# The lead-in of two expert layers: norm by halves, modulation shared with ScalarE, the second head's queries and choice moved forward, tile 1's norm later

## The reference

```python
x = layer_norm(alpha * x + gate1 * mixer(x * (1 + scale1) + shift1))
x = layer_norm(alpha * x + gate2 * peer_ffn(x * (1 + scale2) + shift2))
```

```python
s1, s2 = scores of the two query halves against 128 keys each
v1, i1 = top_k(s1, 16); v2, i2 = top_k(s2, 16)
top_s, pos = top_k(all 256 sums v1 + v2, 16)     # 16 of 16384 experts
gate = softmax(top_s)
act = gelu(dot(t, u_tab[idx]))
out += sum over the 16 of gate * act * v_tab[idx]
```

## Time and profile before

| | |
|---|---|
| runs, median (lowest to highest) | 1878.3 us (1877.2 to 1880.09), 3 runs |
| profiled execution, its own time | 1873.58 us |
| its span, first to last instruction | 1871.8 us |
| mean granted clock of TensorE | 0.980 |
| busy: PE, DVE, ACT, POOL | 1659.1, 1467.1, 601.9, 484.1 us |
| first gather, last gather, layer 0 | 379.56, 1025.13 us |
| first gather, last gather, layer 1 | 1212.25, 1844.74 us |

### The profile page before, as it was taken

How to read it: one execution, slowest core, us unless ns; L and a number is a source line. 1 busy time by engine, 2 the same in 40 slices (tenths; PEclk the granted TensorE clock), 3 DMA queues, 4 the chain that set the end, 5 groups by cost and what they waited for, 6 DMA issues and landing times.

```text
span 1871.8 us, 18240 instructions
## 1 busy us (share of the span) xinstructions
PE 1659.1 (89%) x5432; PEld 907.8 (48%) x5432; DVE 1467.1 (78%) x3511; ACT 601.9 (32%) x1495; POOL 484.1 (26%) x517
## 2 busy tenths in 40 slices
PE   8999999989999987889899998979999878787786
PEld 3787588445544433334343776545454423232332
DVE  6888996787677778898887799787787788777755
ACT  4565854123222223333322111032222323222221
POOL 0000000033333333343343000033333333333341
PEclk9999999999999999999999999989999999999999
DMA  8331239889999999999999685599999999999996
GB/s 356 138 128 59 113 138 370 347 307 420 427 419 427 427 425 417 389 425 427 424 416 428 268 310 225 198 417 422 428 426 426 427 426 419 420 420 426 418 421 273
DMA packets 95846, 664.33 MB, mean 355 GB/s; under 512 B 11357, under 2 KB 13374, under 8 KB 16388
## 3 DMA queue, kind: packets, MB, share of 16 engines
q0 software_dynamic: 73728, 536.90, 68.8%
q1 hardware_dynamic: 22020, 126.27, 17.4%
HBM read 662.02 MB, written 1.11 MB: 354 GB/s over the span
## 4 chain that ended last, share of the span: by engine, by line
PE 34%; DMA 25%; DVE 21%; issue 4%; ACT 2%; PEld 1%; DVEq 0%; POOL 0%; PEldq 0%; POOLq 0%; ACTq 0%
DMA expert_rows<-in_p_uv,chosen_experts 24%; PE bank L1181 19%; DVE dot_products L2497 7%; PE bank L966 3%; PE bank L1139 3%; PE bank L1041 2%; DVE silu_c_row_and_products L1885 1%; PE bank L1392 1%; ACT weight_diagonal L1721 1%; PE bank L981 1%; PEld bank L1181 1%; PE bank L1080 1%; PE bank L1295 1%; PE bank L1211 1%; PE bank L1218 1%
## 5 line engine op out<-in xcount | busy, mean ns | idle before, releaser
L1181 PE MATMUL bank<-expert_rows,weight_diagonal 128*128 128x512 f32 x2048 | 958.1, 612 | 165.3 <-ACT weight_diagonal L1721 163.5
L1432 POOL DMA_INDIRECT expert_rows<-in_p_uv,chosen_experts x512 | 483.7, 945 | 1361.0 <-PE bank L1181 775.8
L2497 DVE SCALAR_TENSOR_TENSOR dot_products<-expert_rows,bank 128x1024 f32<-128x1024 f32 x512 | 625.0, 1221 | 236.0 <-DMA expert_rows<-in_p_uv,chosen_experts 220.9
L1181 PEld LDWEIGHTS bank<-expert_rows,weight_diagonal 128*128 128x128 f32 x2048 | 379.9, 193 | 674.3 <-issue 390.8
L1721 ACT ACTIVATE weight_diagonal<-constants,expert_weights 128x128 f32<-128x128 f32 x512 | 177.8, 394 | 246.0 <-DVE expert_weights L2429 236.8
L1713 ACT ACTIVATE expert_gelu<-expert_dots 128x2 f32<-128x2 f32 x258 | 52.3, 203 | 613.2 <-DVE dot_products L2497 609.6
L926 PE MATMUL bank<-mixer_input_T_hi,weights_hi 128*128 128x512 f32 (+1 forms) x192 | 74.9, 390 | 7.9 <-DVE weights_lo L630 4.7
L2070 DVE SCALAR_TENSOR_TENSOR conv_work_or_state<-conv_work_or_state,channel_vectors 128x252 f32<-128x252 f32 (+2 forms) x192 | 71.9, 429 | 4.0 <-ACT conv_work_or_state L1541 3.9
L926 PE MATMUL bank<-mixer_input_T_hi,weights_lo 128*128 128x512 f32 (+1 forms) x192 | 72.8, 379 | 0.0
L926 PE MATMUL bank<-mixer_input_T_lo,weights_hi 128*128 128x512 f32 (+1 forms) x192 | 72.6, 378 | 0.0
L1311 PE MATMUL bank<-hyena_input_T,hyena_weight_block 128*128 128x256 f32 x320 | 70.5, 379 | 0.0
(11 more groups left out here) (330 smaller groups left out, 1906.3 us busy)
## 6 DMA issues: line engine op xcount, KB each, us to landing
weight_block<-in_ada_rows SPq DMA_DIRECT2D x22, 1024.0 KB, 6.4
weight_block<-in_m_in_blocks SPq DMA_DIRECT2D x20, 1024.0 KB, 6.0
hyena_weight_block<-in_ada_rows SPq DMA_DIRECT2D x15, 1024.0 KB, 7.1
hyena_weight_block<-in_h_in_blocks SPq DMA_DIRECT2D x12, 1024.0 KB, 6.8
weight_block<-in_wq_blocks SPq DMA_DIRECT2D x11, 1024.0 KB, 7.9
expert_rows<-in_p_uv,chosen_experts POOLq DMA_INDIRECT x512
out_weights<-in_m_out_blocks SPq DMA_DIRECT2D x6, 1024.0 KB, 8.1
weight_block<-in_ada_shift SPq DMA_DIRECT2D x4, 1024.0 KB, 11.3
```

The source lines that it names most:

```text
L1181: last = mm(ps[b][:, :], dg[n % DIAG][:, :], uv[slot][:, D + h * 512:D + (h + 1) * 512], start=(r == 0 and k == 0), stop=end)
L1432: pool.indirect_dma_start(uv[slot][:, :], None, A[f"p_uv{l}"], bass.IndirectOffsetOnAxis(ap=chosen[:, s_, k:k + 1], axis=0)).then_inc(uv_l ...
L2497: stt(prod[:, :], uv[slot][:, 0:D], 1.0, rows_t, ALU.mult, ALU.mult, accum_out=dots[:, s_, k + j:k + j + 1]).then_inc(sem("dots_done"), 1)
```

## The change

It has five parts, in both layers unless said.

1. **Halves in the first norm.** The last three row blocks of tile 0's output product are taken half by half, so that bank 0 ends two products ahead of bank 1. VectorE's gate, sum and statistics of half 0 stand ahead of those of half 1. The normalization and the transposes go by halves, with a semaphore for each half. In layer 0 two of the eight modulation dot products move behind the modulation of tile 0 (`LATE_DOTS`), and with them SP's later loads.
2. **ScalarE's share.** ScalarE modulates the second half of tile 0 and both halves of tile 1 (`modulate_half`); VectorE keeps the first half of tile 0. VectorE reads the first head's scores directly from the bank, so ScalarE's two copies go.
3. **The second head's queries at once.** A common `first_head` puts token rows and the second head's queries and scores ahead of most of tile 1's products. In layer 1 the gate rows move behind them all.
4. **The second head's choice** comes ahead of the first unit (pieces 0 to 3), behind the first dot product (4 and 5), and behind the first pair (6 and 7; in layer 1 behind tile 1's norm).
5. **Tile 1's norm later.** In layer 1 it moves behind the second pair of units, as in layer 0; its transposes stand ahead of the combine of unit 4 in both layers (before: of unit 2 in layer 0, of unit 0 in layer 1). In layer 1 the slots of the row buffers are turned by six, so that the first two gathers use buffers that don't wait for the products.

The core of the diff:

```diff
-        mixer_out(0, 0, 6)
+        out_steps = [(k, h) for k in range(INNER // P) for h in range(2)]
+        out_steps_first = out_steps[:-6] + [(k, h) for h in range(2) for k in range(INNER // P - 3, INNER // P)]
...
         def tile_transposes(l, t):
-            pe.wait_ge(sem("layer_norms_done"), TT * 2 * l + t + 1)
             for j in range(2):
+                pe.wait_ge(sem("norm_halves"), 2 * (TT * l + t) + j + 1)
...
+        def first_head(l, out_, steps):
+            out_(1, steps[0:4])
+            tile_transposes(l, 0)
+            out_(1, steps[4:5])
+            first_queries(l, 0, 0, 0, KD)
+            first_queries(l, 0, 1, 0, 4)
+            first_half_scores(l, 0)
+            first_queries(l, 0, 1, 4, KD)
+            token_rows(l, 0, (0,))
+            first_half_scores(l, 1)
+            token_rows(l, 0, (1,))
+            for c in range(2):
+                second_queries(l, 0, c, 0, KD)
+            out_(1, steps[5:7])
+            second_scores(l, 0)
+            out_(1, steps[7:])
...
+        first_head(1, hyena_out, hyena_steps)
         gate_rows(1, 1)
...
-                    if l == 0 and s_ == 0 and k == 2:
-                        tile_transposes(0, 1)
+                    if s_ == 0 and k == 4:
+                        tile_transposes(l, 1)
...
     # GpSimd
                     if n >= UVR:
                         pool.wait_ge(sem("combined"), n - UVR + 1)
+                        if n == UNITS + UVR - FIRST_SLOT[1]:
+                            wait_full(pool, ("hout", 3))
...
-        wait_full(pool, ("hout", 3))
         peer(1)
...
     # ScalarE
+            def modulate_half(t, j):
+                b = wait_full(act, ("tT", l, t, j))
+                for c in range(4):
+                    k = 4 * j + c
+                    last = f(tT[:, k, t * P:(t + 1) * P], ps[b][:, c * P:(c + 1) * P], ACT.Identity, scale=ada[l][:, 4, k:k + 1], bias=ada[l][:, 3, k:k + 1])
+                last.then_inc(read[b], 1)
...
+                    if s_ == 0 and k == (4, 2)[l]:
+                        for j in range(2):
+                            modulate_half(1, j)
...
     # VectorE: ln_stats
+            gated(0)
+            if t == 0:
+                added(0)
+            gated(1)
+            if t:
+                added(0)
+            after(added(1))
...
     # VectorE: choose_first
+                for a in range(2):
+                    b = wait_full(dve, ("sc0", l, 0, a))
+                    scored = ps[b][:, a * P:(a + 1) * P]
+                    after(step(V.max(topv[:, a, 0:8], scored)))
+                    step(V.max_index(topi[:, a, 0:8], topv[:, a, 0:8], scored))
+                    V.match_replace(left[:, a, :], topv[:, a, 0:8], scored, LOWEST).then_inc(read[b], 1)
+                    wait_read(dve, ("sc0", l, 0, a))
+                    after(best(topv[:, a, :], topi[:, a, :], None, left[:, a, :], True))
...
     # VectorE: the units
                 if s_ == 0:
+                    for piece in range(4):
+                        choose(1, piece)
                     gates_of(0)
...
+                        if s_ + k + j == 0:
+                            for piece in (4, 5):
+                                choose(1, piece)
...
-                    if l == 0 and s_ == 0 and k == 2:
+                    if s_ == 0 and k == 2:
                         second_tile()
+                        if l:
+                            for piece in (6, 7):
+                                choose(1, piece)
...
     # SP
-        weights(at("ada1_rows", 6), at(("wq", 0), 3) + 1)
-        ln_rows(0, 0)
+        weights(at("ada1_rows", 6), at(("wq", 0), 2) + 1)
         for h in range(2):
             wait_full(sp, ("gate", 0, 1, h))
         weights(0, 1, query_rings[0])
+        wait_full(sp, ("mout", 1))
+        sp.dma_start(fc[:, 0:FC_COLS], A["filter_constants"]).then_inc(sem("filter_in"), 16)
+        weights(at(("wq", 0), 3), at(("wq", 0), 3) + 1)
+        ln_rows(0, 0)
         wait_read(sp, ("mout", 0))
```

More of the change, by code:

```diff
@@ L88 @@
 UVR = 8
+FIRST_SLOT = (0, UVR - 2)
+LATE_DOTS = 2
 DIAG = 8
@@ L381, in plan_peer @@
         work_, sums = (2, 0) if l else (0, 2)
-        for t in range(TT):
+        for t in range(TT - l):
             for j in range(2):
@@ L391, in plan_peer @@
             plan.use(("sc1", l, 0) if r == 1 else ("sc", l, r, *tiled), 6 + r % 2)
+            if l and r == 1:
+                for h in range(2):
+                    plan.use(("gate", 1, 1, h), 2 + h)
+                for j in range(2):
+                    plan.use(("tT", l, 1, j), 6 + j)
             if l == 0 and r == 3:
@@ L491, in build_in @@
     plan_inv(1, 1)
-    for h in range(2):
-        plan.use(("gate", 1, 1, h), 2 + h)
     for j in range(4):
@@ L1117, in second_scores, with token_rows @@
             last.then_inc(full[b], 1)
-        def token_rows(l, t):
-            for h in range(2):
+        def token_rows(l, t, halves_=(0, 1)):
+            for h in halves_:
                 b = begin(("tn", l, t, h))
@@ L1237, in peer @@
                         filter_products((s_ - PH) // 2, s_ % 2, k)
-                    chunks = ((4, 6, 8, 10), (2, 5, 8, 11))[l] if s_ == 0 else (0, 1, 2, 3)
+                    chunks = (4, 6, 8, 10) if s_ == 0 else (0, 1, 2, 3)
                     if l == 0 and r in BY_TILE:
@@ L1772, in peer @@
                         copy_second_scores(1)
-                    if l == 0 and s_ == 0 and k == 2:
-                        ln_root(0, 0, 1)
-                    if s_ + 2 < PH and k == (10 + 2 * l if s_ == 0 else 4):
+                    if s_ == 0 and k == 2:
+                        ln_root(l, 0, 1)
+                    if s_ == 0 and k == (4, 2)[l]:
+                        for j in range(2):
+                            modulate_half(1, j)
+                    if s_ + 2 < PH and k == (10 if s_ == 0 else 4):
                         copy_queries(s_ + 2)
-                    if s_ + 2 < PH and k == (12 + 2 * l if s_ == 0 else 6):
+                    if s_ + 2 < PH and k == (12 if s_ == 0 else 6):
                         copy_scores(s_ + 2)
@@ L1910, in gate_diagonal, with modulate_tile @@
                ada[l][:, GATES[j], :].unsqueeze(2).to_broadcast([P, KD, P]), ALU.mult).then_inc(sem("gate_diagonals"), 1)
-        def modulate_tile(key, dsts, l, pair, t):
-            for j in range(2):
+        def modulate_tile(key, dsts, l, pair, t, banks_=(0, 1)):
+            for j in banks_:
                 b = wait_full(dve, key + (t, j))
@@ L2301, in ln_norm @@
             after(m)
-            ts(xres[:, t, :], xres[:, t, :], small[:, t, 12:13], small[:, t, 16:17], ALU.subtract, ALU.mult).then_inc(sem("layer_norms_done"), 1)
+            if j:
+                ts(xres[:, t, :], xres[:, t, :], small[:, t, 12:13], small[:, t, 16:17], ALU.subtract, ALU.mult).then_inc(sem("layer_norms_done"), 1)
+            else:
+                for h in range(2):
+                    x = xres[:, t, h * 512:(h + 1) * 512]
+                    ts(x, x, small[:, t, 12:13], small[:, t, 16:17], ALU.subtract, ALU.mult).then_inc(sem("norm_halves"), 1)
         def ln_apply(l, j, t):
@@ L2326, in _ @@
         gate_diagonal(0, 1)
-        for m in range(KD, 2 * KD):
+        for m in range(KD, 2 * KD - LATE_DOTS):
             modulation_dot(1, m)
@@ L2332, in peer @@
         def peer(l, keys):
-            modulate_tile(("tT", l), tT, l, 1, 0)
+            modulate_tile(("tT", l), tT, l, 1, 0, (0,))
+            if l == 0:
+                for m in range(2 * KD - LATE_DOTS, 2 * KD):
+                    modulation_dot(1, m)
             def best(val, idx, src, rest, second):
```

126 lines of the change are left out of this document (39 added, 87 removed).

## The result

The changed kernel takes 1884.6 us (median; 1882.4 to 1885.4), the kernel before, timed with it, 1878.5. The ratio is 1.0037, with an interval of 1.0028 to 1.0046: 0.37% slower, 12 us over the forecast and outside its range. The profiled execution took 1883.73 us (span 1881.9, before 1871.8). The traced execution of the kernel before lies 4.9 us under the median given here, the new one 0.9 under its own, so the two traces lie some 4 us further apart than the medians do.

What follows compares the result with a forecast made beforehand. Fixed-byte DMA plateaus of expert-row gathers bound the kernel, so an earlier stream start moves their end. Gains of 3.7 us in layer 0 and 2.4 in layer 1, together 6.1, take the median from 1878.3 to 1872.2 us; range 1867 to 1877.

Steps and rivals of the forecast that it cites:

- The 2.23 us ahead of the transposes: Layer 0, TensorE: norm by halves removes this idle time, so transposes can start at 360.7.
- the queries wait: Layer 0, TensorE: first queries wait 0.2 us for tile 0's modulated first half, 362.9 against TensorE free at 362.8.
- the second head's 0.77: Layer 0, TensorE: second head's queries wait 0.9 us (0 to 2) for the bank of scores VectorE reads itself.
- combine 4 starts: Layer 0, TensorE: starts at 405.3 instead of 410.39, so the thirteenth gather is issued at 407.2 instead of 412.65.
- The price that the Trainium skill gives for reading a bank: VectorE's direct score reads: skill implies 0.4 us more per layer, time 0.8 later; prediction took at most 0.04 each as nothing.
- the 2.4 us set against them: Layer 1's start: gain by 1260, taken between 3.2 us and 1.9 us with half a gather of unexplained shortfall.
- its rival: Only the start moves: layer 1's two gathers ahead (5.0) less the third's delay gives 1.8 us; chance 0.20.
- its second term: Layer 1's gain of 2.4 us, from two gathers near 1207 and the third issued at 1215.4.
- The step that failed: Layer 1: tile 1's norm delays combines of units 4 on, but not past the stream's need; buffers last until 1237.
- the prediction's signs of being wrong: TensorE's combines waiting for diagonals at 410, idle above 3 us before second queries, or a lower-rate plateau.
- Only the start moves: Rival: something else keeps buffers late behind the products; gain 0.9 plus 1.8, together 2.7 us, 1875.6; chance 0.20.
- The bank that VectorE must empty: Rival: TensorE waits before second queries in each layer; gain 6.1 - 2d, gone at d = 3.1; chance 0.08.

Runs made afterwards that it cites:

- kernel 4: Changed kernel with layer 1's orders, banks, copies and first buffer as before, so mainly layer 0's lead-in changed; 0.9982 of the kernel before.
- kernel 10: Changed kernel with only ScalarE's modulation of tile 1 in layer 1 moved behind the diagonals of units 4 and 5; 1.0010 of the kernel before.
- Kernel 12: Changed kernel with layer 1's norm a pair sooner, third head's copies later, last two choice pieces behind units 2 and 3; 0.9968 of the kernel before, median 1869.8 us.
- kernel 5: Changed kernel with, in layer 1, tile 1's norm a pair sooner and the third head's copies later, banks shared; 0.9963 of the kernel before.
- kernel 6: Changed kernel with, in layer 1, tile 1's norm a pair sooner, the third head's copies later and separate accumulator banks; 0.9970 of the kernel before.
- kernel 8: Changed kernel with layer 1's late norm kept, separate banks, third head's copies later, last two choice pieces and modulation behind later units; 0.9965 of the kernel before.
- kernel 9: Changed kernel with only layer 1's last two pieces of the second choice moved behind units 6 and 7; 1.0036 of the kernel before.
- Kernel 3: Changed kernel with layer 1's third-head copies later, queries behind units 12 and 13, scores behind 14 and 15; 1.0011 of the kernel before.
- kernel 2: Changed kernel with layer 1's tile 1 norm, transposes and root one pair of units sooner, banks shared; 1.0010 of the kernel before.

## Why the prediction was wrong

**Layer 0, right.** Its steps came out within half a microsecond. (Bank 0 of tile 0 ends three products ahead of bank 1, two earlier than before.) TensorE, the last row the combine of unit 4, and then VectorE's second MAX8 from a bank (for the earlier trace rows):

```profile
360.40 1.12 PE L1078 MATMUL bank<-constants,x_residual 128*128 128x128 f32 x8 [0.25 <-DVE x_residual L2322]
...
362.61 2.92 PE L1089 MATMUL bank<-t_T,weight_block 128*128 128x128 f32 x24 [0.23 <-DVE t_T L1925]
...
368.70 3.81 PE L1115 MATMUL bank<-t_T,weight_block 128*128 128x128 f32 x32 [0.77 <-DVE scores_left L2417]
...
404.81 1.98 PE L1190 MATMUL bank<-expert_rows,weight_diagonal 128*128 128x512 f32 x4 [0.93 <-ACT weight_diagonal L1719]
```
```profile
367.60 0.30 DVE L2415 MAX8 top_values<-bank 128x8 f32<-128x128 f32 x1
```

The 2.23 us ahead of the transposes shrank to 0.25; the queries wait 0.23 (forecast 0.2), the second head's 0.77, released by VectorE's MATCH_REPLACE8 (0.9); combine 4 starts at 404.8 (405.3). That the times agree to a few tenths is in part luck: in the traces of all thirteen kernels with this layer 0 the seventh gather issues between 393.5 and 396.5 and the last between 1019.9 and 1024.6, so the 3.9 us of one pair of traces are known to some 2 us. The waits are what bears the account: in the traces of kernels 4, 10 and 12 they are the same within 0.01. The price that the Trainium skill gives for reading a bank ("VectorE: DVE Perf Modes", the section on the TRN2 errata), an estimate of 65 ns an instruction by its cycles, does not show: MAX8 takes 0.30 from the bank, 0.29 from SBUF.

**Layer 1, its start: right in time, too large in worth.** Layer 1 lies 3.9 us earlier. With that added the first three gathers are at 1207.3, 1208.6 and 1216.4, forecast about 1207 and 1215.4. But the 2.4 us set against them took a part of before's own shortfall of half a gather as gained: by streams that don't stall the forecast times give 1.8, as its rival has it. And the third gather comes 1.0 later than forecast, so the two early gathers put the new stream only 0.8 us ahead: 12 gathers end at 187.1 + 1.7 + 12 x 2.48 = 218.6 from layer 0's last gather before, at 191.3 + 1.7 + 10 x 2.48 = 217.8 after. Kernel 12's thirty-third gather is 0.8 ahead by the table, and level if counted from layer 0's last gather. The timed runs do not settle this term: kernels 5, 6, 8 and 12 lie 0.0012 to 0.0019 (2 to 4 us) under kernel 4, whose layer 1 is the old one, but the intervals overlap. That the sum of the repaired kernels comes so near the forecast is therefore not a proof of its second term.

**The step that failed** is the last sentence of the prediction's paragraph on layer 1: "Tile 1's norm, now behind the second pair, delays the combines of units 4 and on, but not past the stream's need: eight buffers from 1217.1 last until 1237 and longer." The need was sized, the delay was not. Measured, the thirteenth gather is 5.1 us past the need, and layer 1 loses 10 us where it was to gain 2.4. Added up as in layer 0 it was there to be found: not the norm alone stands between units 3 and 4, but, in layer 1 only, the last two pieces on VectorE and the modulation on ScalarE ahead of the gelu of units 4 and 5 (in layer 0 behind it). Combine 4 comes 14.5 us after combine 0, in layer 0 8.8 (395.97 to 404.81). Kernel 10 prices the modulation, with the table load behind it, at 5 us, kernel 9 the pieces alone at nothing. None of the prediction's signs of being wrong looked at the combines of layer 1.

**The step that was left out:** the third head's copies, which the change moves from behind units 12 and 14 to 10 and 12 in layer 1 and which neither the list of the change's parts names nor the prediction prices. They make ScalarE wait for TensorE, which is late with the query products, 13.4 us, and hold the gelu of units 12 and 13 behind them. Kernel 3 prices this at 5 us by itself; on top of kernel 2 it is 0.0047 (kernel 5), 9 us, each ratio being uncertain by 0.0011 to 0.0016. The change also moves the third head's query products on TensorE in layer 1, from behind combines 2, 5, 8 and 11 to behind 4, 6, 8 and 10. They stay there in kernels 3, 5 and 12, so their new places by themselves cost nothing that shows.

**The rivals.** "Only the start moves" named ScalarE's modulations and TensorE's query chunks. The modulations are one of the two losses of layer 1, and the chunks are what ScalarE's early copy waited for; but it gave them the worth of a gain not made, not of a loss. The bank that VectorE must empty cost 0.77 us a layer and did not decide. The other bank, the accumulators over tile 1's products, was in no rival.

**The sum.** Forecast 3.7 + 2.4 gained. The traces have 3.9 gained in layer 0 and 14.1 lost behind it (from layer 0's last gather to layer 1's: 819.6 before, 833.7 after), 10.1 as the spans have it. By the timed runs, which the 4 us between the traced executions do not touch, it is 6.9 lost, made of 3.4 gained (kernel 4) and 10.3 lost.

## What to carry to other kernels

When a block of work is moved into a queue, go through every engine that the block has a share on and add up what then stands ahead of the next item that frees a buffer; the engine whose queue ends last sets the price, and trimming another one (kernel 9) buys nothing until that one is shorter. A pattern that is right in one layer need not be in the next: compare the places of each follower, the copies and modulations too, and not only of the block. And a full stream keeps its lateness: what was lost by its thirty-third gather (14.3 us, counted from layer 0's last) is still lost at its last (14.1). In the twelve edited kernels the two agree to some 3 us.

## What was not expected of the hardware

After such gaps TensorE's clock is at its lower level, which adds to what they cost. In the changed kernel (stretches, columns as above, and a later combine):

```profile
1233.00:1238.00 5.00, 0.67 (x7) 0.43 (x4) 1.59 (x6) 4.48 (x11) 0.94 (x1) 0.98 0.97 349
1238.00:1243.00 5.00, 4.64 (x7) 2.40 (x8) 4.52 (x8) 1.50 (x5) 0.59 (x1) 0.50 0.73 310
```
```profile
1265.15 3.62 PE L1190 MATMUL bank<-expert_rows,weight_diagonal 128*128 128x512 f32 x4 [2.82 <-ACT weight_diagonal L1719]
```

After an idle time of 4.69 us the granted clock from 1238 to 1243 is 0.50, the lower level of 1.2 GHz, and the first four combine records take 3.78 us. After 2.82 us idle the same four take 3.62 (granted clock 0.50 from 1265.15 to 1268), after 1.57 us idle (kernel 10) 1.99. So the late gelu cost 1.8 us more on TensorE than its own lateness. In the same way combines 0 to 3 take 8.90 us after 10.42 us of idle time, with a granted clock of 0.50 from 1223.9 to 1226.9; in layer 0, with no idle time ahead of them and a clock of 1.00, 7.03.

A switch of ScalarE's function table costs 1.28 us of the engine and no more here: the modulation ends at 1236.17, the load runs from 1236.18 to 1237.46 and the gelu starts at 1237.47. The Trainium skill ("ScalarE: Activation LUTs", the section on what ACT_TABLE_LOAD costs) has the same 1283 ns and a drain of some 1380 ns on top; no idle time of that kind stands around the load here.
